# Experts of three token tiles by streaming whole tables, the last tile by gathering rows

## What is computed

```python
q = (xb @ w_q).reshape(T, 8, 2, 128)              # 8 heads, two halves
s = einsum('thpd,hpkd->thpk', q, sub_keys)        # 2 x 128 scores a head
sv, si = top_k(s, 16)                             # 16 of each half
cand = sv[:, :, 0, :, None] + sv[:, :, 1, None]   # 256 candidates
top_s, pos = top_k(cand, 16)
idx = key pair of pos                             # 16 experts of 16384
gate = softmax(top_s)
act = gelu(einsum('thkd,td->thk', down[idx], xb))
out = einsum('thk,thkd->td', gate * act, up[idx])
```

## Time and profile before

| | |
|---|---|
| median of 3 runs | 3461.99 us (3461.6 to 3464.84) |
| span of the profiled execution | 3459.0 us |
| TensorE, VectorE, ScalarE, GpSimd busy | 57%, 58%, 20%, 60% |
| mean granted TensorE clock | 0.736 |
| moved by DMA | 1167 MB, 337 GB/s over the span |

### The profile page before, as it was taken

The page is one execution under the profiler, slowest core; times in us unless marked ns, Lnnn a source line. Parts: engine busy times, 40 slices in busy tenths (PEclk is TensorE's granted clock), DMA queues, the critical chain, the costliest instruction groups (busy, mean ns, idle before and its releaser), DMA issues.

```text
span 3459.0 us, 30792 instructions
## 1 busy us (share of the span) xinstructions
PE 1958.3 (57%) x10149; PEld 1019.7 (29%) x10149; DVE 2003.2 (58%) x4999; ACT 674.6 (20%) x1905; POOL 2070.7 (60%) x2099
## 2 busy tenths in 40 slices
PE   8998997444444444434279684544445444343675
PEld 3554654222222222212034352222222222221221
DVE  1243427777777777766511157777777777676210
ACT  3011213111121121111131112121211111111231
POOL 1313214777777777766665226777777777677573
PEclk9999788666566666665689797666666666656798
DMA  6223146999999999999998759999999999999995
GB/s 234 73 73 110 49 158 244 410 409 409 409 400 409 409 405 405 402 409 401 377 366 288 265 188 351 409 409 409 409 409 406 403 409 403 405 399 408 351 393 220
DMA packets 338224, 1167.08 MB, mean 337 GB/s; under 512 B 37114, under 2 KB 40468, under 8 KB 336916
## 3 DMA queue, kind: packets, MB, share of 16 engines
q0 software_dynamic: 294912, 1073.87, 79.1%
q1 hardware_dynamic: 43156, 91.26, 7.2%
HBM read 1162.90 MB, written 2.10 MB: 337 GB/s over the span
## 4 chain that ended last, share of the span: by engine, by line
DMA 31%; POOL 25%; PE 19%; issue 10%; DVE 8%; ACT 1%; POOLq 0%; DVEq 0%; ACTq 0%
PE banks L778 16%; DMA scr<-in_peer_down,idx 14%; DMA scr<-in_expert_u,idx 14%; POOL ring L729 12%; POOL scr L717 12%; DVE scr L2080 5%; PE banks L1125 3%; DMA ring<-in_expert_v,idx_v 1%; DMA scr<-in_expert_v,idx_v 1%; POOL scr L729 1%; DMA const<-in_peer_up,idx_v 1%; DMA ring<-in_peer_up,idx_v 1%; ACT hT L1348 0%; DVE ring L2048 0%; DVE ring L2045 0%
## 5 line engine op out<-in xcount | busy, mean ns | idle before, releaser
L2080 DVE CUSTOM_DVE_ANT_0 scr<-scr,banks 128x1024 f32<-128x1024 f32 x1024 | 1223.8, 1219 | 575.3 <-DMA scr<-in_peer_down,idx 281.6
L1125 PE MATMUL banks<-ring 128*32 128x512 f32 x3712 | 675.3, 864 | 1167.0 <-DMA ring<-in_peer_up,idx_v 551.9
L717 POOL DMA_INDIRECT scr<-in_expert_u,idx x512 | 488.0, 953 | 324.5 <-DVE scr L2080 126.9
L717 POOL DMA_INDIRECT scr<-in_peer_down,idx x512 | 487.0, 951 | 264.2 <-DVE scr L2080 124.0
L1125 PEld LDWEIGHTS banks<-ring 128*32 128x32 f32 x3712 | 136.4, 138 | 1546.1 <-issue 1460.5
L729 POOL DMA_INDIRECT ring<-in_peer_up,idx_v x464 | 436.8, 941 | 179.4 <-issue 144.0
L729 POOL DMA_INDIRECT ring<-in_expert_v,idx_v x464 | 436.6, 941 | 162.1 <-issue 144.8
L778 PE MATMUL banks<-ring,scr 128*128 128x128 f32 (+1 forms) x2112 | 393.7, 368 | 4.6 <-ACT ring L1498 4.6
L778 PEld LDWEIGHTS banks<-ring,scr 128*128 128x128 f32 x2112 | 366.5, 271 | 23.4 <-issue 19.2
L689 POOL TENSOR_TENSOR ring<-ring,silu 128x4096 f32<-128x4096 f32 x8 | 56.2, 7022 | 312.5 <-DMA ring<-in_w_mod 312.5
L778 PE MATMUL banks<-ring,hT 128*128 128x512 f32 x512 | 234.7, 618 | 14.6 <-DVE X L1976 11.8
(11 more groups left out here) (232 smaller groups left out, 2214.5 us busy)
## 6 DMA issues: line engine op xcount, KB each, us to landing
ring<-in_w_mod SPq DMA_DIRECT2D x12, 2048.0 KB, 8.0
ring<-in_w_in SPq DMA_DIRECT2D x7, 2048.0 KB, 12.8
scr<-in_peer_w_q SPq DMA_DIRECT2D x1, 8192.0 KB, 28.0
scr<-in_peer_down,idx POOLq DMA_INDIRECT x512
scr<-in_w_q SPq DMA_DIRECT2D x4, 2048.0 KB, 7.9
scr<-in_expert_u,idx POOLq DMA_INDIRECT x512
ring<-in_peer_up,idx_v POOLq DMA_INDIRECT x464, 11.2
ring<-in_expert_v,idx_v POOLq DMA_INDIRECT x464, 11.2
```

The costliest lines, as they stand in the source:

```text
L717: nc.gpsimd.indirect_dma_start(u_rows[:, k % SLOTS, :], None, table_u, bass.IndirectOffsetOnAxis(idx[:, n % IDX_SLOTS, k:k + 1], 0)).then_ ...
L1125: last = nc.tensor.matmul(psum[2 + c][32 * g:32 * g + 32, :], spread[:, n % 2, k, :], up_rows[slot + g][:, c * CW:(c + 1) * CW], start=(h ...
L2080: V.tensor_tensor_reduce(u_rows[:, k % SLOTS, :], u_rows[:, k % SLOTS, :], xn, 1.0, 0.0, ALU.mult, ALU.add, dots[:, n % 2, k:k + 1]).then_ ...
```

## The change

In both layers the experts of tiles 0, 1 and 2 (`DENSE = 3`) are no longer gathered. All 16,384 experts are computed for these 384 tokens, in 128 blocks of 128 experts:

- a block of `down` (512 KB, plain DMA from SP) is turned by 8 transposes, copied by ScalarE, and multiplied with `hT[:, :, 0:384]`: 8 products of 384 columns; ScalarE's gelu writes the hidden values;
- VectorE multiplies them with the block's gates (`weigh`);
- a block of `up` is multiplied with the result into six PSUM banks that stay open for the whole loop: 3 tiles x 2 halves, 512 columns each (`add_up`).

The gates come from a table of 16,384 x 384 values, zero but for the chosen experts, in HBM (`gates_out`). It is built during routing: for 16 tokens at a time GpSimd makes 16 matrices (one-hot of the first key times the gate, `picks_a`, 16 operations of 128 columns), VectorE one of 16 x 128 (one-hot of the second key, `picks_b`), TensorE multiplies them (`gate_table`, 16 products of 128 columns, four banks), ScalarE copies the banks, and SP writes 1 MB. During the dense loop SP reads it back, 1.5 MB for 8 blocks. The first 32 hidden blocks are computed during routing, the others three steps ahead of their use.

Tile 3 still gathers: 2 x 128 indirect DMAs a layer, 8 slots, with dot products (TENSOR_TENSOR_REDUCE) and weighted sums both on VectorE, spread over steps 21 to 126. The query weights are streamed by heads. The routing loop goes tile by tile; queries of tile 2 are computed together with tile 3's. The rests of the overlap between stages (`beside`, `late_*`, `EARLY`) are removed: the second mixer works on all 512 columns after the stage. `Iota` is kept with 128 columns and the quad constants go.

The core of the diff (TensorE's and VectorE's programs in particular; what is left out is the same work in ScalarE's program, buffers, and removed code):

```diff
+DENSE = 3
+DW = DENSE * P
+N_ROUTE = TT * PH
+N_BATCH = DENSE * PH
+AHEAD = 32
+LEAD = 3
+DN_SLOTS = 3
+UP_SLOTS = 4
+WQ_SLOTS = 3
+SCORE_SLOTS = 3
+GROUP = 8
+N_GROUPS = NKEYS // GROUP
+STEADY = 10
+ROW_SLOTS = 8
+N_ROWS = 2 * PH * TOPK
+ROWS_FROM = 21
...
+HIDDEN_IN_STEP = ((1, 1, 1, 1, 1, 1, 1, 1), (1, 1, 1, 2, 1, 1, 1, 2), (1, 1, 1, 2, 1, 1, 1, 2), (1, 0, 1, 0, 1, 0, 1, 0))
+LATE_SCORES = {0: 30, 4: 31}
+ROW_HEADS = [("D", 0)] + [x for h in range(1, PH) for x in (("D", h), ("U", h - 1))] + [("U", PH - 1)]
...
+            def picks_a(layer, t, b):
+                m = t * PH + b
+                if b == 0:
+                    empty(pool, "KT", layer, t)
+                if m > 0:
+                    full(pool, "G", layer, (m - 1) // PH, (m - 1) % PH, 3)
+                for q in range(16):
+                    tok = 16 * b + q
+                    last = nc.gpsimd.tensor_scalar(pick_a[:, q, :], iota, pick_keys[:, 0, tok:tok + 1], pick_keys[:, 2, tok:tok + 1],
+                                                   ALU.is_equal, ALU.mult)
+                last.then_inc(a_set, 1)
...
+            def queries(layer, i):
+                t, h = divmod(i, PH)
+                n = layer * N_BATCH + i
+                pe.wait_ge(wq_in[i % WQ_SLOTS], 16 * (n // WQ_SLOTS + 1))
+                w = w_q[i % WQ_SLOTS]
+                o = begin("q", layer, i)
+                width = P if t < DENSE - 1 else 2 * P
+                for half in range(2):
+                    for k in range(KT):
+                        last = mm(o[:, half * width:(half + 1) * width], w[:, k, half * P:(half + 1) * P],
+                                  hT[:, k, t * P:t * P + width], k, KT)
+                last.then_inc(bank_ready, 1)
...
+            def hidden_of(layer, c, turn_next):
+                if turn_next:
+                    turned(layer, c + 1, 0)
+                empty(pe, "T", layer, c, 1)
+                o = take("H", layer, c)
+                for k in range(KT):
+                    if turn_next and k == 4:
+                        turned(layer, c + 1, 1)
+                    last = mm(o[:, 0:DW], dT[:, c % 2, k, :], hT[:, k, 0:DW], k, KT)
+                done("H", layer, c)
+                last.then_inc(bank_ready, 1)
...
+            def gate_table(layer, t, b):
+                n = layer * N_BATCH + t * PH + b
+                pe.wait_ge(a_set, n + 1)
+                pe.wait_ge(b_set, n + 1)
+                for j in range(4):
+                    o = begin("G", layer, t, b, j)
+                    for q in range(4):
+                        last = mm(o[:, q * P:(q + 1) * P], pick_b[:, 4 * j + q, :], pick_a[:, 4 * j + q, :], 0, 1)
+                    last.then_inc(bank_ready, 1)
...
+            def add_up(layer, c):
+                n = layer * NKEYS + c
+                pe.wait_ge(weighted, n + 1)
+                pe.wait_ge(up_in[n % UP_SLOTS], 16 * (n // UP_SLOTS + 1))
+                g = hidden(c)
+                for t in range(DENSE):
+                    for half in range(2):
+                        last = nc.tensor.matmul(psum[2 * t + half][:, :], g[:, t * P:(t + 1) * P],
+                                                up_rows[n % UP_SLOTS][:, half * CW:(half + 1) * CW],
+                                                start=(c == 0), stop=(c == NKEYS - 1))
+                    if c == NKEYS - 1 and t < DENSE - 1:
+                        last.then_inc(acc_done, 1)
+                last.then_inc(up_done, 1)
+            def routing(layer):
+                for i in range(N_ROUTE):
+                    t, h = divmod(i, PH)
+                    if t < DENSE:
+                        scores(layer, i + 2)
+                        if i + 3 < N_BATCH:
+                            queries(layer, i + 3)
+                    elif h % 2 == 0:
+                        scores(layer, N_BATCH + 2 + h // 2)
+                    for c in hidden_in_step(i):
+                        hidden_of(layer, c, c + 1 < AHEAD)
+                    if t >= 1:
+                        if h == 0:
+                            pick_cols(layer, t - 1)
+                        gate_table(layer, t - 1, h)
+            def dense(layer):
+                for u in range(NKEYS):
+                    if u in LATE_SCORES:
+                        scores(layer, LATE_SCORES[u])
+                    if u in (6, 7):
+                        last_rows(layer, u - 6)
+                    c = u + LEAD
+                    if AHEAD <= c < NKEYS:
+                        if c == AHEAD:
+                            for half in range(2):
+                                turned(layer, c, half)
+                        hidden_of(layer, c, c + 1 < NKEYS)
+                    if layer == 1 and u >= NKEYS - 2:
+                        p_cols(u - (NKEYS - 2))
+                    if u == 0:
+                        drained(range(2 * DENSE))
+                    add_up(layer, u)
...
+            def picks_b(layer, t, b):
+                m = t * PH + b
+                if b == 0:
+                    empty(dve, "KT", layer, t)
+                if m > 0:
+                    full(dve, "G", layer, (m - 1) // PH, (m - 1) % PH, 3)
+                V.tensor_tensor(pick_b, iota.unsqueeze(1).to_broadcast([P, 16, P]),
+                                pick_keys[:, 1, 16 * b:16 * (b + 1)].unsqueeze(2).to_broadcast([P, 16, P]), ALU.is_equal
+                                ).then_inc(b_set, 1)
...
+            def weigh(layer, c):
+                g = layer * N_GROUPS + c // GROUP
+                if c % GROUP == 0:
+                    dve.wait_ge(gate_in[g % 2], 16 * (g // 2 + 1))
+                empty(dve, "H", layer, c)
+                V.tensor_tensor(hidden(c), hidden(c), g_in_buf[g % 2][:, :, c % GROUP], ALU.mult).then_inc(weighted, 1)
...
+            def row_op(layer, r):
+                kind, h = ROW_HEADS[r // TOPK]
+                k, slot = r % TOPK, r % ROW_SLOTS
+                done = layer * N_ROWS + r
+                if kind == "U" and k == 0:
+                    dve.wait_ge(gelu_done, layer * PH + h + 1)
+                    V.tensor_tensor(weight[:, h, :], gelu[:, h, :], gate[:, h, :], ALU.mult).then_inc(row_weight, 1)
+                    dve.wait_ge(row_weight, layer * PH + h + 1)
+                if r == 0:
+                    empty(dve, "xr", layer, 1)
+                dve.wait_ge(row_in[slot], 16 * (done // ROW_SLOTS + 1))
+                if kind == "D":
+                    V.tensor_tensor_reduce(rows[slot], rows[slot], xn_last, 1.0, 0.0, ALU.mult, ALU.add, dots[:, h, k:k + 1]
+                                           ).then_inc(row_used, 1)
+                elif h == 0 and k < 2:
+                    V.tensor_scalar(row_sum[k], rows[slot], weight[:, h, k:k + 1], None, ALU.mult).then_inc(row_used, 1)
+                else:
+                    dve.wait_ge(row_used, done - 1)
+                    V.scalar_tensor_tensor(row_sum[k % 2], rows[slot], weight[:, h, k:k + 1], row_sum[k % 2], ALU.mult, ALU.add
+                                           ).then_inc(row_used, 1)
+            def dense(layer):
+                last_routes = {2: lambda: route(layer, 28), 5: lambda: route(layer, 29), 8: lambda: keys_of(layer, TT - 1, 2),
+                               11: lambda: route(layer, 30), 14: lambda: route(layer, 31)}
+                for u in range(NKEYS):
+                    weigh(layer, u)
+                    if u in last_routes:
+                        last_routes[u]()
+                    if u == 15:
+                        softmax_shift(layer, TT - 1)
+                    if u == 17:
+                        keys_of(layer, TT - 1, 3)
+                    if u == 20:
+                        softmax(layer, TT - 1)
+                    for r in range(rows_upto(u - 1), rows_upto(u)):
+                        row_op(layer, r)
```

More of the change, by code:

```diff
@@ L332, in gates @@
+    open_layer(1, "wo2", "gf")
+    routing(1)
+    dense(1)
     def gates(t):
@@ L1967, in _, with add_projection @@
             dve.wait_ge(gains_done, 3)
[L1969 to L1971 removed]
+            def add_projection(layer, name, t):
+                for n in range(2):
                     o, x = full(dve, name, t, n), X[:, t, n * CW:(n + 1) * CW]
```

1681 lines of the change are left out of this document (786 added, 895 removed).

## The result

The changed kernel takes **4644.7 us** (median of four runs, 4641.4 to 4647.8) where the kernel before takes 3461.8 (3459.8 to 3464.8): a ratio of 1.342, 95% interval 1.340 to 1.344. Forecast were 4315 us and a range of 4200 to 4540. The sign was right; the size was off by 330 us, and the time lies above the range. The profiled execution spans 4645.9 us.

What follows compares the result with a forecast made beforehand. DMA gathers bound the kernel before, TensorE after. Sum: 564 until routing, two layers of 1709 (routing 440, start 20, dense loop 1249), middle 235, tail 95: 4312, plus 3 gives 4315 us; range 4200 to 4540.

Steps and rivals of the forecast that it cites:

- What bounds before and after: Expert stages before: DMA fetching 1024 blocks a layer (537 MB); after: 318 MB, DMA no longer the bound, TensorE's work instead.
- Prices on TensorE and the dense step: Dense loop: 512-wide matmul 0.863 us, eight of 384 columns 5.18 (5.36 in a row with a weight switch), full step 11.28.
- Wide matmuls overlap in a long stream: Rival, dense loop: 512- and 384-wide matmuls run 1.48 times faster or more, near 3180 us at 1.65 times; 2%.
- Start, middle, tail: Outside routing and dense streaming: 20 us of idle TensorE before each dense loop, 235 us between layers, 95 us at the end.
- The gathers hold the dense loop: Rival, dense loop: the last tile's 256 gathers, in order with VectorE's products, set its time; 4400 us or more; 4%.
- GpSimd's picks: Routing: 16 one-input operations of 128 columns a step, 5 us a step, from 2.5 as low end to 10 as high.
- The loop of picks and gate matmuls: Routing: single pick buffers make a loop of 3.6 + 5 + 0.3 = 9 us, hidden until step 20, then +23 us.
- clock falls in routing: Rival, routing: picks' waits keep TensorE at 1.2 GHz, up to 399 us more a layer; 4415, at worst 5100 us; 12%.
- A clock under 0.9: Sign of being wrong: TensorE's clock under 0.9 in either stage, routing or dense loop.
- signs of being right: Dense loops: TensorE over 98% busy, clock 1.00, steps 11.2 to 11.4 us, DMA near 0.5; routing 420 to 500 a layer.
- GpSimd's picks set the pace: Rival, routing: picks at 10 us a step make the loop 14, +50 us a layer; 4410 to 4530 us; 20%.
- VectorE slowed beside GpSimd: Part of the 20% picks rival, routing: VectorE's two-input operations slowed, as 0.69 us became 2.34; up to 60 us more.

## Why the forecast was right in its sign and wrong in its size

- **What bounds before and after**: right. The DMA share fell from 1.02 to 0.62, and TensorE took its place.
- **Prices on TensorE and the dense step**: right to 1% (11.19 for 11.28; 1244 to 1246 for 1249). Sizing 384 columns at three quarters of the 512-wide price, rather than from the row with a switch in it, was the better choice: 5.16 us measured for 5.18.
- **Wide matmuls overlap in a long stream**: refuted. 1244 us at 100% busy, clock 1.00, ran at 0.43 us a record as the 14 us of the earlier trace rows did.
- **Start, middle, tail**: 17 for 20, 212 for 235, 87 for 95. These estimates were all a little high, and with the dense loops (8 us) they hid some 44 us of the miss.
- **The gathers hold the dense loop**: no. VectorE's operations and GpSimd's issues had room.
- **GpSimd's picks: the step that failed.** "5 us" a step, with 10 as high end, is 14.5 in the timeline. The term was sized from a select and an add of 512 columns, scaled by columns with a small fixed part. Measured were 0.79 us a pick, 0.44 of it for 128 columns, and 1.8 us more a step behind VectorE's comparison. So the high end was no bound: both rows had the same width, and neither operation was a pick's. The add's other widths, which the trace had, would have given 0.41 us.
- **The loop of picks and gate matmuls**: the mechanism was right, the size and the place were not. Forecast was 9 us a step, felt in the last eight steps only. At 20.7 it is above TensorE's 10 to 17 us in most steps. Layer 0's 189 us over forecast are, within a microsecond: three tile starts of 17.1, 16.5 and 15.2 us for 18 in all (+31); waits of 87 us in the last seven steps for 23 (+64); waits of 55 us in the other steps for none (+55); TensorE's own work 438 us for 399 (+39). Of the 55 us 11 are no picks at all but the two waits for ScalarE's exponential, a dependence that the sum didn't have. The handover in halves took 88 us a layer off with the same picks, so the loop over single buffers is a cost beside their length.
- **The clock**: that last term is the "clock falls in routing" rival in a small form. After a wait for picks the 32 gate records ran at a mean clock of 0.62, without a wait before them at full clock (two windows of the changed kernel, at 1146.2 and at 929.1 us):

```profile
1146.20:1151.90 5.70, 5.70 (x32) 5.70 (x33) 0.00 (x0) 1.79 (x3) 0.00 (x0) 0.62 0.01 3
929.10:932.70 3.60, 3.60 (x34) 3.60 (x33) 0.00 (x0) 2.28 (x4) 0.00 (x0) 1.00 0.03 11
```

The 24 steps' gate matmuls take 131 us instead of 86. The clock is a consequence of the waits: the picks on VectorE in halves, which end most of them, also brought it back, from 0.84 over routing to 0.96. A clock under 0.9 was one of the forecast's own signs of being wrong, and routing of 629 us lies outside the 420 to 500 of its signs of being right; the signs for the dense loop came true, but for the DMA share (0.62, not near 0.5).

- **The rival "GpSimd's picks set the pace"** (20%, 4410 to 4530 us) was the case that came true, priced by the same two rows and so 115 us too low at its top. Its second part, VectorE slowed beside GpSimd, read a mean for a price (0.69 us became 7.30 once, not 2.34); here it was GpSimd's first pick that was held. The range ended where that rival's price did.

## What to carry to other kernels

A short operation on GpSimd can't be priced by dividing another wide one by its columns. Look for one operation at several widths, which gives the fixed part; if no row shows the operation itself, let the high end be a whole wide one (here the add's 1.30 us, which would have held). Where one set of buffers is handed back and forth between engines, write the loop's length beside the work of every step, not only of the last, and count the clock that TensorE loses after each wait. And price one unit (here, a tile of tokens) on the engine that it leaves and on the one that it goes to, 350 against 400 us, and then what each design costs without any unit. Here the units are 300 us of the 1183 lost, and the part that doesn't shrink with them is most of the rest.

## What was not expected of the hardware

- GpSimd's two-operation compare and multiply on 128 columns takes 0.79 us (0.57 with 64 columns, 0.60 with the comparison alone), longer than its select on 512 columns (0.635), while VectorE does the same sixteen as two operations of 2.29 us.
- VectorE's two-input operation and one of GpSimd exclude each other, whichever is second: 2.89 us for a 0.79-us pick, and 7.30 for a 0.69-us product on VectorE.
- The kernel before took 3459, 4049 or 4037 us depending on the chip; the kernel bound by TensorE took 4644.7 and 4648.7 us on two of these. A comparison of a kernel bound by gathers with one that is not holds for its chip: the same change is 34% slower on one and 16% on another.
